# Gated delta net in a two-block model: one stream of projection products for the whole stage, and a new order of squares, outputs and convolutions

## What is computed

```python
proj = (u @ w_in)                     # among others gq, gk, gv, gz, gate_g
qkv = silu(causal_short_conv(concat([gq, gk, gv]), conv_w))     # 4 taps
q_g = l2norm(cq) * GDN_DK ** -0.5 ; k_g = l2norm(ck)            # 8 heads, each used by 2 value heads
# per chunk: A = strict_tril(kb k^T * Lmat); T = inverse(eye + A)
# v_new = u - w S ; o = q exp(gam) S + (q k^T * Lmat) v_new ; S = S exp(g_end) + k_to_end^T v_new
o_g = rmsnorm(o_g, gdn_out_norm) * silu(gz)
y_g = o_g @ w_branch_gdn ; y = sigmoid(gate_h) * y_h + sigmoid(gate_g) * y_g
```

## Time and profile before

| | |
|---|---|
| median of 3 runs | 2895.38 us (2893.43 to 2896.52) |
| profiled execution, its time | 2897.22 us |
| its span | 2895.3 us |
| PE busy | 2773.5 us (96%) |
| DVE busy | 1276.8 us (44%) |
| ACT busy | 619.1 us (21%) |
| POOL busy | 43.0 us (1%) |
| share of PE in the chain that ended last | 85% |

### The profile page before, as it was taken

The page is one execution under the profiler, slowest core; times in us unless marked ns, Lnnn a source line. Parts: engine busy times, 40 slices in busy tenths (PEclk is TensorE's granted clock), DMA queues, the critical chain, the costliest instruction groups (busy, mean ns, idle before and its releaser), DMA issues.

```text
span 2895.3 us, 29431 instructions
## 1 busy us (share of the span) xinstructions
PE 2773.5 (96%) x11772; PEld 1852.3 (64%) x11772; DVE 1276.8 (44%) x2536; ACT 619.1 (21%) x1426; POOL 43.0 (1%) x73
## 2 busy tenths in 40 slices
PE   8999898998999999999999989999999999999999
PEld 5445557656468888746465745555555586688886
DVE  3723232335234456335464254554545343344554
ACT  2123221236210000223333021313232301100001
POOL 0000000000000000000000000010101000000000
PEclk9999899998999999999999998989898999999999
DMA  4111012100122222211110312121202132122221
GB/s 150 58 59 59 30 60 77 59 30 1 58 88 87 88 88 80 80 58 59 58 56 33 118 37 73 44 80 37 88 29 95 73 124 87 59 88 88 87 88 73
DMA packets 124975, 201.47 MB, mean 70 GB/s; under 512 B 8172, under 2 KB 64296, under 8 KB 123944
## 3 DMA queue, kind: packets, MB, share of 16 engines
q1 hardware_dynamic: 120784, 181.15, 18.3%
q0 software_dynamic: 3792, 18.35, 2.0%
q10 hardware_dynamic: 264, 0.10, 0.0%
HBM read 189.10 MB, written 10.49 MB: 69 GB/s over the span
## 4 chain that ended last, share of the span: by engine, by line
PE 85%; DVE 7%; DMA 3%; ACT 2%; issue 2%; POOL 1%; ACTq 0%; DVEq 0%; SPq 0%; POOLq 0%
PE psum L506 18%; PE psum L503 14%; PE psum L2216 10%; PE psum L416 9%; PE psum L436 7%; PE psum L401 6%; PE psum L2198 5%; PE psum L1140 2%; PE psum L2079 2%; DVE arena L3040 1%; DVE arena L3038 1%; PE psum L634 1%; PE psum L1160 1%; PE psum L1148 1%; PE psum L389 1%
## 5 line engine op out<-in xcount | busy, mean ns | idle before, releaser
L2216 PE MATMUL psum<-weight_ring,h_t 128*128 128x512 f32 x896 | 406.8, 599 | 0.5 <-issue 0.5
L2216 PEld LDWEIGHTS psum<-weight_ring,h_t 128*128 128x128 f32 x896 | 164.2, 192 | 171.7 <-issue 170.8
L559 DVE TENSOR_TENSOR arena<-arena,psum 128x512 f32<-128x512 f32 x179 | 122.9, 687 | 336.8 <-PE psum L506 280.0
L2198 PE MATMUL psum<-h_t,weight_ring 128*128 128x512 f32 x512 | 250.8, 638 | 8.1 <-ACT arena L2566 7.9
L416 PE MATMUL psum<-h_t,weight_ring 128*128 128x512 f32 x560 | 246.9, 602 | 9.3 <-DMA weight_ring<-in_w_in_dram 5.6
L506 PE MATMUL psum<-h_t,weight_ring 128*128 128x256 f32 x1024 | 228.2, 379 | 0.0
L503 PE MATMUL psum<-weight_ring,arena 128*128 128x256 f32 x992 | 220.2, 379 | 1.5 <-ACT arena L2594 1.5
L506 PEld LDWEIGHTS psum<-h_t,weight_ring 128*128 128x128 f32 x1024 | 194.5, 190 | 27.5 <-issue 1.3
L503 PEld LDWEIGHTS psum<-weight_ring,arena 128*128 128x128 f32 x992 | 188.4, 190 | 27.7 <-issue 2.2
L416 PEld LDWEIGHTS psum<-h_t,weight_ring 128*128 128x128 f32 x560 | 107.3, 193 | 144.5 <-issue 134.6
L401 PE MATMUL psum<-weight_ring,h_t 128*128 128x512 f32 (+3 forms) x512 | 180.3, 508 | 0.8 <-DVEq L1586 0.8
(11 more groups left out here) (402 smaller groups left out, 3390.8 us busy)
## 6 DMA issues: line engine op xcount, KB each, us to landing
weight_ring<-in_ffn_w_in_dram SPq DMA_DIRECT2D x44, 1024.0 KB, 7.2
weight_ring<-in_w_in_dram SPq DMA_DIRECT2D x20, 2048.0 KB, 7.7
weight_ring<-in_ffn_w_out_dram SPq DMA_DIRECT2D x8, 2048.0 KB, 7.8
weight_ring<-in_w_in_even_dram SPq DMA_DIRECT2D x7, 2048.0 KB, 8.1
weight_ring<-in_w_in_odd_dram SPq DMA_DIRECT2D x5, 2048.0 KB, 7.8
weight_ring<-in_w_in_dram SPq DMA_DIRECT2D x8, 1024.0 KB, 7.0
weight_ring<-in_w_branch_gdn_dram SPq DMA_DIRECT2D x4, 2048.0 KB, 10.2
weight_ring<-in_ffn_w_out_dram SPq DMA_DIRECT2D x4, 1536.0 KB, 6.8
```

The source lines that it names most:

```text
L559: ins = dve.tensor_tensor(out, other, bank, op)
L2198: last = pe.matmul(bank, slot[:, k, n * P:(n + 1) * P], act[:, k, :], start=(k == 0), stop=(k == KD - 1))
L2216: last = pe.matmul(bank, act[:, k, t * P:(t + 1) * P], slot[:, k, :], start=(k == 0), stop=(k == KD - 1))
```

## The change

All projections of the delta net become one generator, `pe_gdn_stream`, in the old order of blocks, and every step takes products from it. It runs ahead: `LEAD` = 12 products of the group's `gv` are done before its sums of squares. What stands between the steps changes so:

- **PE.** Before the first sums 12 products instead of 8; in a later group none between the last `do` and the sums, where there were 10 (beside 2 that belong to the last step). Between the sums and the second pair of `kq` 10 products instead of 8; after them 4, then `k_tok`, 6, values 0 and 1 transposed, all 32 of `gz`, values 2. Values 3 are transposed after `x5`. In the inverse 16 products instead of 8, in the state 28 instead of 22. Behind the last step of group 3, 20 remain instead of 34.
- **Squares** of tiles 2 and 3 lie in `c_v`, not in `sq`, so that all four can be made before the sums; the semaphore between them goes.
- **ACT.** Padding copies of the next group come earlier (tile 0 and 1 in the inverse), outputs of the group before come ahead of the decays, silu of tiles 6 and 7 and values 2 after all four silus of `gz`; in group 3 the sigmoids of `gate_g` take the places of the padding copies.
- **DVE.** Reciprocals come ahead of the outputs of the group before; convolution 4 and 5 stand where 5 and 6 did, 6 and 7 after the solve; in the state loop the next group's convolution stands ahead of the output of the tile before, not behind it.

```diff
+    fill = pe_gdn_stream(K, pe, s)
+    pe_take(fill, LEAD)
     for g in range(4):
-        pe_gdn_prepare(K, pe, s, V, g)
-        pe_gdn_inverse_and_state(K, pe, s, V, g)
-    pe_take(pe_stream_token(K, pe, (s, "gate_g", 1), K.h_t), NT * KD)
+        pe_gdn_prepare(K, pe, s, V, g, fill)
+        pe_gdn_inverse_and_state(K, pe, s, V, g, fill)
+    pe_take(fill, NT * KD)
     pe_gdn_outputs(K, pe, s, V, 3)
...
+LEAD = 12
...
+    for g in range(4):
+        yield from pe_stream_feature(K, pe, (s, "gv", g), K.h_t)
+        yield from pe_stream_token(K, pe, (s, "gz", g), K.h_t)
+        if g < 3:
+            yield from pe_stream_feature(K, pe, (s, "gqk", g + 1), K.h_t)
+    for half in range(2):
+        yield from pe_stream_token(K, pe, (s, "gate_g", half), K.h_t)
...
-    fill = pe_stream_feature(K, pe, (s, "gv", g), K.h_t)
-    pe_take(fill, KD)
     bank = pe_fresh(K, pe, (s, "sums", g))
...
-    pe_take(fill, 2 * KD)
-    fill = pe_stream_token(K, pe, (s, "gz", g), K.h_t)
-    for n in range(4):
-        pe_take(fill, KD)
-        pe.wait_ge(K.conv_silu, 8 * g + 5 + n)
-        pe_transpose(K, pe, (s, "v_tok", g, n), lambda t, n=n: V["c_v"][:, n % 2, t * P:(t + 1) * P])
+    pe_take(fill, 4 * KD - LEAD - 14)
+    for n in range(2):
+        pe_gdn_values(K, pe, s, V, g, n)
+    pe_take(fill, 4 * KD)
+    pe_gdn_values(K, pe, s, V, g, 2)
...
         last.then_inc(K.full_of((s, "x5", g, p)), 1)
-    pe_take(fill, 2)
+    pe_gdn_values(K, pe, s, V, g, 3)
+    pe_take(fill, 4)
...
         last.then_inc(K.full_of((s, "vn", g, j)), 1)
-        pe_take(fill, 2)
+        pe_take(fill, 3 if j else 2)
...
         last.then_inc(K.full_of((s, "do", g, j)), 1)
-        pe_take(fill, 2)
-    pe_take(fill, 64)
+        pe_take(fill, 3 if j else 2)
...
 def act_gdn_square(K, act, s, V, g, n):
     act.wait_ge(K.conv_silu, 8 * g + n + 1)
-    if n >= 2:
-        act.wait_ge(K.sums_read, 3 * g + n - 1)
...
+    act.activation(gdn_squares(V, n), V["c_qk"][:, 4 * (g % 2) + n, :], ACT.Square).then_inc(K.squared, 1)
...
-    dve_gdn_conv(K, dve, s, V, g, 5)
+    dve_gdn_conv(K, dve, s, V, g, 4)
...
-    dve_gdn_conv(K, dve, s, V, g, 6)
+    dve_gdn_conv(K, dve, s, V, g, 5)
     dve.wait_ge(K.blocks_in, 16 * (g + 1))
...
     dve.tensor_copy(bm.rearrange("p (c i) -> p i c", c=32), bt.rearrange("p (i c) -> p i c", c=32)).then_inc(K.blocks_solved, 1)
+    dve_gdn_conv(K, dve, s, V, g, 6)
     dve_gdn_conv(K, dve, s, V, g, 7)
...
                 dve.tensor_tensor(decayed, state, ends, ALU.mult).then_inc(K.one_more("dve"), 1)
+            if g < 3:
+                dve_gdn_conv(K, dve, s, V, g + 1, j)
             dve_gdn_output(K, dve, s, V, g, j - 1)
-        if g < 3:
-            dve_gdn_conv(K, dve, s, V, g + 1, j)
+        elif g < 3:
+            dve_gdn_conv(K, dve, s, V, g + 1, 0)
```

More of the change, by code:

```diff
@@ L2268, in pe_gdn_prepare @@
         for j in range(NT):
[L2269 removed]
+            last = pe.matmul(bank[:, 4 * n + j:4 * n + j + 1], gdn_squares(V, n)[:, j * P:(j + 1) * P],
                              K.const("ones")[:, 0:1], start=True, stop=True)
[L2271 to L2274 removed]
+    last.then_inc(K.full_of((s, "sums", g)), 1)
     pe_take(fill, 4)
@@ L2289, in pe_gdn_prepare @@
     for pair in ((0, 1), (2, 3)):
-        if pair[0]:
-            pe_gdn_decays(K, pe, s, V, g, pair)
+        pe_gdn_decays(K, pe, s, V, g, pair)
         for j in pair:
@@ L2552, in act_gdn, with act_gdn_gate, act_gdn_following @@
     for t in range(NT):
-        key = ((s, "gate_g", 1), t)
-        act.wait_ge(K.full_of(key), K.turn(key))
-        act.activation(V["gate_g1"][:, t, :], K.bank(key), ACT.Sigmoid).then_inc(K.free_of(key), 1)
+        act_gdn_gate(K, act, s, V, NT + t)
     act_gdn_outputs(K, act, s, V, 3)
+def act_gdn_gate(K, act, s, V, tile):
+    half, t = tile // NT, tile % NT
+    key = ((s, "gate_g", half), t)
+    act.wait_ge(K.full_of(key), K.turn(key))
+    act.activation(V[f"gate_g{half}"][:, t, :], K.bank(key), ACT.Sigmoid).then_inc(K.free_of(key), 1)
+def act_gdn_following(K, act, s, V, g, tile):
+    if g < 3:
+        act_gdn_pad(K, act, s, V, g + 1, tile)
+    else:
+        act_gdn_gate(K, act, s, V, tile)
 def act_gdn_pad(K, act, s, V, g, n):
@@ L2574, in act_gdn_conv_silu @@
         dst = V["c_v"][:, n % 2, :]
-        if n >= 6:
+        if n < 6:
+            act.wait_ge(K.full_of((s, "sums", g)), K.turn((s, "sums", g)))
+        else:
             act.wait_ge(K.full_of((s, "v_tok", g, n - 6)), K.turn((s, "v_tok", g, n - 6)))
@@ L2581, in act_gdn_square @@
     act.wait_ge(K.conv_silu, 8 * g + n + 1)
-    if n >= 2:
-        act.wait_ge(K.sums_read, 3 * g + n - 1)
-    act.activation(V["sq"][:, n % 2, :], V["c_qk"][:, 4 * (g % 2) + n, :], ACT.Square).then_inc(K.squared, 1)
+    if g and n < 2:
+        act.wait_ge(K.full_of((s, "sums", g - 1)), K.turn((s, "sums", g - 1)))
+    if g and n >= 2:
+        act.wait_ge(K.full_of((s, "v_tok", g - 1, n)), K.turn((s, "v_tok", g - 1, n)))
+    act.activation(gdn_squares(V, n), V["c_qk"][:, 4 * (g % 2) + n, :], ACT.Square).then_inc(K.squared, 1)
 def act_gdn_outputs(K, act, s, V, g):
```

75 lines of the change are left out of this document (36 added, 39 removed).

## The result

The changed kernel takes 2869.14 us (median of 4 runs, 2864.88 to 2871.64); the kernel before, in the same set, 2895.95 us (4 runs, 2893.43 to 2902.57). The ratio is 0.9902, with a 95% interval of 0.9882 to 0.9923. The profiled execution took 2871.64 us, with a span of 2869.8 us.

A forecast was written before the change was run, and what follows sets the result against it. PE, busy 96%, was taken as the bound, with gains only from its waits and low clock. Period 31.4 + 40.9 + 3.7 + 68.3 = 144.3 us; saved 22.8 - 2.9 - 0.6 = 19.3, from 2895.4 to 2876; range 2862 to 2891.

The forecast's parts named there:

- State loop: Loop with 28 products instead of 22: 40.9 us, 39.1 in group 3; the 4.2 us wait of `ks` goes.
- the waits on `v_new`: In the state loop, `su` waits for ACT's copy behind DVE's later output: 1.2 us at j = 2, 0.6 at j = 3.
- Inverse: From `x5` on, with 16 products instead of 8 and one transpose: 31.4 us in all four groups, bounds 28.5 and 39.
- The two products more ahead of `r6`: In the inverse, two added products ahead of `r6` cost 1.7 us.
- The block ahead of `x6`: In the inverse, four new products ahead of `x6` cost 5.3 us, between 3.4 (high clock) and 7.4 (low).
- the lower bound (28.5): Shortest inverse allowed for, in us, if the clock holds after the first block.
- Sums to `x5`: Stretch from the sums to `x5`: sums 3.7 us, then 68.3, of which 24.2 to the last `lower` and 44.1 behind it.
- the clock no longer falls at the sums: Four products behind the sums cost 3.4 us, not 5.27, as PE need not wait 0.62 us there: 1.8 less.
- The wait before `x5`: PE's wait for the DMA of the inverse blocks: about 6 us, four times, 25 us in all; idle time grows.
- filled everywhere: Rival: sums to `x5` shortens to PE's own 59 us, total 2840; chance 0.12 together with an inverse near 28.5.
- Start: Group 0 does four more products before its first sums, 3.4 us later, chain to `x5` 0.5 shorter: 2.9 lost.
- End: From `x5` of group 3 to the next stage: 91.0 us instead of 90.45, 0.6 lost.

The follow-up runs named there:

- e2: Changed kernel with DVE's output of the tile before put back ahead of the next group's convolution in the state loop: 2861.41 us, ratio 0.9887.
- e5: Changed kernel with one of the four products that follow the sums put behind each quarter of them: 2862.43 us, ratio 0.9880.
- e1: Kernel before with 14 instead of 8 products in the inverse, ACT and DVE in their old order: 2873.22 us, ratio 0.9922.
- e7: Changed kernel with 22 of the 31 steps of the solve, so its inverse is incomplete: 2840.36 us, ratio 0.9806.
- e4: Changed kernel with LEAD = 6 instead of 12 and two products at each place of the state loop: 2859.84 us, ratio 0.9872.
- e10: e9 with ACT's padding copy of tile 5 moved from between decays 1 and 2 to behind decay 3: 2836.86 us, ratio 0.9797.
- e9: Changed kernel with LEAD = 3, output ahead of convolution, sums interleaved with products, 18 products in the inverse, 17 in the state loop: 2862.15 us, ratio 0.9866.

## Why the prediction came out as it did

The direction, the size (2876 forecast, 2869.14 measured) and the range were right, and so was the mechanism in the main: the state loop loses its wait, fewer matmuls run at the low clock, and the wait before `x5` grows. That the total is so near is in part luck, since the two terms that were off lie on opposite sides. By the terms of the sum:

- **State loop**, forecast 40.9 us, measured 40.8. The wait on the new state went, and the waits on `v_new` came where they were worked out, a little smaller: 0.90 and 0.31 us where I had 1.2 and 0.6. e2 shows their cause.
- **Inverse**, forecast 31.4, measured 29.0 on average (29.33, 29.12, 28.64, 28.78): the term that was mis-sized most, 9.7 us over four groups. The two products more ahead of `r6` were put at 1.7 us and cost 0.1: in group 3 two took 3.63 us before, nearly all of it at the low clock, and four take 3.70 at the high one in every group. That is 6.4 of the 9.7 us. The block ahead of `x6` was put at 5.3; it took 3.70 in groups 2 and 3 and 5.40 in groups 0 and 1. I had let the clock come back one step too late; it is back by `t5` in all four. That is why the lower bound (28.5) was nearly met.

  In groups 0 and 1 the clock then fell once more, behind `t5` and `r5`, with nothing waiting. Group 1 in the changed kernel: the block in PE's timeline, then the windows of `t5` with `r5` and of the block.

```profile
1929.78 5.40 PE L2198 MATMUL psum<-h_t,weight_ring 128*128 128x512 f32 x8
```

```profile
1925.91:1929.78 3.87, 3.87 (x130) 3.83 (x129) 0.70 (x1) 1.17 (x2) 0.00 (x0) 1.00 1.05 403
1929.78:1935.10 5.32, 5.32 (x11) 2.02 (x8) 0.69 (x1) 0.00 (x0) 0.00 (x0) 0.68 0.12 43
```

- **Sums to `x5`**, forecast 72.0, measured 73.6 to 74.4. The step that failed is "the clock no longer falls at the sums": I gave 1.8 us for it, blaming the 0.62 us wait before them. The wait went and the clock fell all the same, only later: the scales stood 9.7 to 11.0 us behind the start of the sums before and stand 8.7 behind it now. e5 shows that the unbroken row of one-column matmuls does it. It cost 1.7 us in each of groups 1 to 3. From the end of the sums to the last `lower` of group 1 it is 25.9 us, as before (25.8), not 24.2.
- **The wait before `x5`**, forecast some 6 us in each group, 25 in all; measured 23.8 us, longest 6.4. That idle time stays equal or grows while the kernel gets faster was the main claim, and it held. The rival "filled everywhere" fell with it.
- **Start**, forecast 2.9 us lost: the sums of group 0 stand 3.5 us later and `x5` 0.3 nearer, 3.2. **End**, forecast 91.0 from `x5` of group 3, measured 88.4, which is the inverse's 2.6. The wait of 1.5 us for ACT stood as before, and DVE's last weight sum ended at 2292.3, 0.7 us before PE went on (2293.00).

So 19.3 us were forecast for the delta net and 23.4 came: 9.7 more from the inverse, 5.7 less from sums to `x5`, and next to nothing in all the others. A further 2.1 us of the profiled run lie ahead of the delta net and are not the change's; e2 had 7.0 us less there. The delta net starts at 1675 to 1685 us in the kept traces, though the program ahead of it is the same.

A reading that the numbers did not expose, but e1 did: I told the gain as the work of all parts together, with squares moved so that the sums need not wait. Moving six products on PE alone gives it. What the new order on ACT and DVE and the twelve products ahead bring and cost comes out even: the chain to `x5` is 1 to 2 us shorter than in e1, the loop 0.8 longer, and the wait at `x5` 12 us longer in all (23.8 against 11.3).

The Trainium skill (TensorE: Matmul & The Clock Gate, Why this matters for your kernels) names idle gaps as what takes the clock down. For the wait before `x5` the runs agree (e7: 1.7 instead of 23.8 us of wait, and 26.4 instead of 29.0 us for the inverse). For the sums they show a second way, without any gap (8.7 us from sums to scales, 7.07 when products break the row up, e5).

## What to carry to other kernels

Filler work is worth most in the stretch whose chain it does not lengthen. So find, for each stretch between two dependences, whether PE waits at its end; move filler from the stretches that have none into that one, and stop when the wait is gone (e4, e10). Look at what each move makes late in the *other* engines' queues: a copy with no urgency in front of an urgent instruction becomes a wait as soon as its producer is moved back (e9).

Spread filler so that each run of small matmuls has a dense block beside it. The same 16 products in blocks of four gave inverses of 28.1 to 29.6 us, and as 2, 2, 2 and 10 of 30.0 to 37.8.

## What the runs showed of the hardware

- A row of 16 matmuls with one output column each (32 records, 3.63 us at the high clock) takes the granted clock down in most cases, with no wait before or in it: 21 times of 28. The four products behind it then take mostly 5.2 to 6.5 us instead of 3.7. With one product behind every eight records the clock stays up (21 times of 21).
- The same may happen among the 32x32 steps of the inverse. In groups 0 and 1 of the changed kernel `t5` and `r5` ran at the high clock, nothing waited, and the four products behind them took 5.40 us. In e10, group 1, even `x5` (2.11 us) and the four products behind it (3.60) were at the high clock before the next four took 5.04. In e7 they took 3.70 in the same place. In the eleven kernels that have four products there it happened in 16 of 44 inverses; what decides it stays open.
- A wait of 5.7 to 6.4 us before `x5` costs 0.9 to 4.4 us more than itself (2.6 on average, changed kernel against e7).
